# Gate products among the linear mixers, norms inside the output loop, and five smaller moves in a two-block decoder

## The reference

```python
h = rms_norm(x) * (1.0 + scale) + shift                 # modulation from c @ w_ada
(qa, ka, va, lra, ga, qb, fb, ib, gb, qc, kc, vc, gc) = split_columns(h @ w_in)
log_alpha = log_sigmoid(lra @ w_gla_gate2 + b_gla_gate) / 16
o_a = rms_norm(chunk_gated_linear_attn(qa, ka, va, log_alpha)) * gla_norm_w * silu(ga)   # "a", 512 wide
o_b = rms_norm(chunk_gated_linear_attn(silu(qb), k_b, ib, log_f)) * hgrn_norm_w * silu(gb)  # "b", 256 wide
o_c = stick_breaking_attn(qc, kc, vc) * silu(gc)                                          # "stick", 256 wide
x = x + gate * (concatenate([o_a, o_b, o_c]) @ w_out)
x = rms_norm(x) * final_norm_w
```

```python
x = x + memory_cross_attention(rms_norm_2(x, norm_cross), ...)
x = x + hierarchical_moe(rms_norm_2(x, norm_ffn), ...)   # router, then 32 experts of 512
return rms_norm_2(x, norm_final)
```

## Time and profile before

| | |
|---|---|
| median of 3 runs | 2309.74 (2307.14 to 2310.19) |
| the profiled execution, its own time | 2315.48 |
| its span, first to last instruction | 2313.6 |
| mean granted TensorE clock | 0.959 |
| PE, DVE, ACT, POOL busy | 93%, 37%, 24%, 11% of the span |
| last slices (experts): DMA | 408 to 414 GB/s |

### The profile page before, as it was taken

The page is one execution under the profiler, slowest core; times in us unless marked ns, Lnnn a source line. Parts: engine busy times, 40 slices in busy tenths (PEclk is TensorE's granted clock), DMA queues, the critical chain, the costliest instruction groups (busy, mean ns, idle before and its releaser), DMA issues.

```text
span 2313.6 us, 38071 instructions
## 1 busy us (share of the span) xinstructions
PE 2144.2 (93%) x15826; PEld 1198.3 (52%) x15826; DVE 863.6 (37%) x1488; ACT 552.5 (24%) x1002; POOL 249.7 (11%) x252
## 2 busy tenths in 40 slices
PE   6998899887998998999999899999899999999997
PEld 4445555555333443654445544466556666666553
DVE  2206630654555341185545563124421111111114
ACT  3013222323652210144112311023111111111112
POOL 0005410442330000000000000000010000000002
PEclk9998999987998999999999999999899999999999
DMA  8121121104010206102110302010389999999995
GB/s 296 61 94 53 37 64 37 46 14 141 1 71 20 64 35 209 37 1 73 37 37 1 137 0 73 0 49 37 137 296 409 412 408 414 410 411 411 409 368 225
DMA packets 100149, 348.98 MB, mean 151 GB/s; under 512 B 18632, under 2 KB 48992, under 8 KB 87264
## 3 DMA queue, kind: packets, MB, share of 16 engines
q1 hardware_dynamic: 56496, 267.64, 29.6%
q0 software_dynamic: 14688, 54.53, 6.3%
q10 hardware_dynamic: 28880, 25.66, 3.4%
HBM read 308.75 MB, written 39.06 MB: 150 GB/s over the span
## 4 chain that ended last, share of the span: by engine, by line
PE 38%; DMA 9%; DVE 4%; issue 1%; ACTq 0%; ACT 0%; POOL 0%; POOLq 0%; DVEq 0%; PEldq 0%
PE bank L590 17%; PE bank L1167 9%; DMA y_of_slot<-HT 9%; PE bank L1183 5%; PE bank L1001 2%; DVE work L1741 1%; PE bank L646 1%; PE bank L1173 1%; PE bank L1158 1%; PE bank L1253 1%; DVE HT L1776 1%; ACTq L1669 0%; PE bank L975 0%; ACT work L1277 0%; PE bank L1107 0%
## 5 line engine op out<-in xcount | busy, mean ns | idle before, releaser
L590 PE MATMUL bank<-slots,HT 128*128 128x512 f32 (+3 forms) x1216 | 427.2, 509 | 3.6 <-DVE HT L1776 1.9
L590 PE MATMUL bank<-HT,slots 128*128 128x512 f32 x736 | 320.8, 598 | 3.8 <-PEq L580 1.3
L590 PEld LDWEIGHTS bank<-slots,HT 128*128 128x128 f32 x1216 | 213.7, 195 | 196.6 <-issue 187.9
L1277 ACT ACTIVATE work<-bank 128x512 f32<-128x512 f32 (+5 forms) x215 | 114.4, 537 | 506.1 <-PE bank L590 352.5
L590 PEld LDWEIGHTS bank<-HT,slots 128*128 128x128 f32 x736 | 141.0, 192 | 181.3 <-issue 176.5
L1277 ACT ACTIVATE work<-work 128x1024 f32<-128x1024 f32 (+7 forms) x199 | 160.3, 817 | 246.7 <-DVEq L141 161.1
L1277 ACT ACTIVATE HT<-bank 64x256 f32<-64x256 f32 (+2 forms) x234 | 100.7, 435 | 462.5 <-PE bank L1167 221.6
L1167 PE MATMUL bank<-slots,HT 128*32 128x256 f32 x3264 | 179.5, 379 | 2.3 <-DVE HT L2366 1.2
L2446 POOL TENSOR_TENSOR work<-work 128x1024 f32<-128x1024 f32 (+4 forms) x84 | 137.0, 1630 | 379.6 <-DVEq L141 313.0
L1167 PE MATMUL bank<-work,HT 128*32 128x256 f32 x3072 | 168.9, 379 | 0.0
L1167 PEld LDWEIGHTS bank<-slots,HT 128*32 128x32 f32 x3264 | 107.6, 110 | 72.3 <-issue 6.1
(11 more groups left out here) (260 smaller groups left out, 2349.4 us busy)
## 6 DMA issues: line engine op xcount, KB each, us to landing
slots<-in_w_e_gate_dram SPq DMA_DIRECT2D x17, 2048.0 KB, 18.1
slots<-in_w_e_up_dram SPq DMA_DIRECT2D x17, 2048.0 KB, 22.7
slots<-in_w_e_down_dram SPq DMA_DIRECT2D x17, 2048.0 KB, 23.4
work<-in_w_e_gate_dram SPq DMA_DIRECT2D x16, 2048.0 KB, 18.0
work<-in_w_e_up_dram SPq DMA_DIRECT2D x16, 2048.0 KB, 22.7
work<-in_w_e_down_dram SPq DMA_DIRECT2D x16, 2048.0 KB, 23.5
slots<-in_w_in_dram SPq DMA_DIRECT2D x9, 2048.0 KB, 8.1
y_of_slot<-HT ACTq DMA_DIRECT2D x132, 96.0 KB, 23.4
```

The lines of the kernel that those rows point to most:

```text
L590: ins = pe.matmul(bank, lhsT, rhs, start=(n == 0), stop=(n == len(pairs) - 1))
L1277: return act.activation(o, i, f, bias=bias, scale=scale, **more)
```

## The change

1. *Gates of a made ahead.* `a_gate`'s products leave the output stage. Two tiles are made in `linear("a")`, six in `linear("b")`; each of the four pairs now has 56 products ahead (before 48, 48, 32, 32). All of them go to one HBM tensor, `products_ahead`.
2. *Where stick's inputs live.* Q and K come back through the weight slots as a chunk (`stick_qk`); the values go to `HT[:, 4:6]`, the gates of a to `HT[:, 0:4]`, of b to `HT[:, 6:8]`, all loaded by SP after the chunk `out1`, in pieces of 128 columns. The gates of stick follow when the linear stages are over, the chunk `att_q` when the stick stage is.
3. *Log-sigmoid under values.* The running sums' loop becomes a function, `running_sums(pair)`. `a_rank` comes before `a_v`; the bias products stand behind the first tile of values, seven tiles follow. Copies of values move behind the log-sigmoid on ACT and behind the running sums of the first pair on DVE, in a and b.
4. *Norms in the output loop.* Mean squares of tiles 0 and 1 are taken at the end of the stick stage and rooted with Ln and Exp; the other tiles' norm is `mix_normed(i + 2)` inside the loop over tiles. The gates of a and b lie in HT by tile columns (`gates[:, :, i * P:(i + 1) * P]`) and are multiplied as before; the norm weights `gla_w`, `hgrn_w` (now one column each) are applied in ACT's copy of the turned tile.
5. The router products of a step stand behind the turn of tile n-3; ACT squares a tile before it copies logits.
6. POOL waits for the first gathered block before it issues the second gather.
7. `BY_DVE = (2, 5, 7)`.

```diff
         add_chunk("a_qk_still")
+        add_chunk("a_rank", (w_in, 1024, 1040))
         add_chunk("a_v", (w_in, 512, 1024))
-        add_chunk("a_rank", (w_in, 1024, 1040))
         for n in range(4, 6):
             add_chunk(f"ada{n}", (w_ada, 512 * n, 512 * n + 512))
         add_chunk("c_qk", (w_in, 2576, 3088))
         add_chunk("c_gate", (w_in, 3344, 3600))
+        add_chunk("a_gate", (w_in, 1040, 1552))
         add_chunk("b_qf", (w_in, 1552, 2064))
         add_chunk("b_v", (w_in, 2064, 2320))
+        add_chunk("a_gate_still")
         add_chunk("cv_bgate", (w_in, 3088, 3344), (w_in, 2320, 2576))
-        add_chunk("a_gate", (w_in, 1040, 1552))
+        ahead_dram = scratch("products_ahead", [P, 28 * HALF])
+        add_chunk("stick_qk", (cut(ahead_dram[:, 0:4 * T], NK), 0, HALF))
...
-                 "b": [("cv_bgate", i, None) for i in range(NT)]}
-        AHEAD_CALLS = {"a": (8, 4, 4, 4, 4, 4, 4, 4, 3, 2, 7), "b": (6, 3, 3, 3, 3, 3, 3, 3, 2, 1, 2)}
+                 + [("c_gate", m, half) for m in range(2) for half in range(2)]
+                 + [("a_gate", i, None) for i in range(2)],
+                 "b": [("cv_bgate", i, None) for i in range(NT)] + [("a_gate", i, None) for i in range(2, NT)]}
+        EVEN = (6, 5, 5, 5, 5, 5, 5, 5, 4, 4, 7)
+        AHEAD_CALLS = {"a": (EVEN, (12, 8, 4, 4, 4, 4, 4, 4, 3, 3, 6)), "b": (EVEN, (11, 8, 4, 4, 4, 4, 4, 4, 4, 3, 6))}
         AHEAD_FIRST = {"a": 0, "b": len(AHEAD["a"])}
         ahead_over = {"a": [], "b": []}
-        AHEAD_GATES = 4 * T
-        AHEAD_ROWS = AHEAD_GATES + 4 * HALF
-        ahead_dram = scratch("stick_inputs", [P, AHEAD_ROWS + NT * HALF])
+        GATES_AHEAD = cut(ahead_dram[:, 4 * T:4 * T + 4 * HALF], 4)
+        A_AHEAD = [(0, 2, cut(ahead_dram[:, 12 * HALF:14 * HALF], 2)), (2, NT, cut(ahead_dram[:, 22 * HALF:28 * HALF], 6))]
+        B_AHEAD = cut(ahead_dram[:, 14 * HALF:22 * HALF], NT)
...
+        A_GATES, B_GATES = HT[:, 0:4, :], HT[:, 6:8, :]
...
+            ranked = ringA.filled
+            product_tm("a_v", 512, tm_fills()[0:1])
+            pe.wait_ge(ringA.free, ranked)
             Q, K, G, V, E, Qe, Ke, S = lin_area()
             for m in range(2):
                 for half in range(2):
                     ringV.close(pe.matmul(ringV.open(pe), Ke[0][0:RANK, m * P:(m + 1) * P],
                                           Ke[1][0:RANK, half * HALF:(half + 1) * HALF], start=True, stop=True))
+            product_tm("a_v", 512, tm_fills()[1:])
...
+            stick_over.append(4 * phases[0])
+            idle_products(banks[7], 5)
+            hear("dve")
+            turn_tile(0, O[:, 0, :], ringA, SB0 // P)
+            turned = [ringA.filled]
             for i in range(NT + 1):
+                if i + 1 < NT:
+                    hear("dve")
+                    turn_tile(i + 1, O[:, i + 1, :], ringA, SB0 // P)
+                    turned.append(ringA.filled)
                 if i < NT:
-                    product_tm("a_gate", 512, [(i, ringA)])
+                    pe.wait_ge(ringA.free, turned[i])
+                    for name in ("out0", "out1"):
+                        w = weights(name)
+                        ringV.close(chain(ringV.open(pe), [(mixed(k, i), w[:, k, :]) for k in range(NK)]))
+                        used(name)
                 if i:
                     hear("dve")
-                    turn_tile(i - 1, O[:, i - 1, :], ringA, SB0 // P)
-            emptied()
-            projected(("out0", "out1"), NORMED, 1, mixed)
+                    turn_tile(i - 1, NORMED[(i - 1) % 2], ringV)
...
-                for i in ROUTED_AT.get(n, ()):
-                    pe.wait_ge(ringV.free, turned_banks[i])
-                    router_product(i, ringA)
                 if n >= 3:
                     normed_ready.hear(pe)
                     turn_tile(n - 3, NORMED3[n % 3], ringV)
                     turned_banks.append(ringV.filled)
+                for i in ROUTED_AT.get(n, ()):
+                    pe.wait_ge(ringV.free, turned_banks[i])
+                    router_product(i, ringA)
...
+            do(rstd[:, 0:16], rstd[:, 0:16], ACT.Ln)
+            do(rstd[:, 0:16], rstd[:, 0:16], ACT.Exp, scale=-0.5)
             tell("dve")
-            hear("dve")
-            do(rstd[:, :], rstd[:, :], ACT.Sqrt)
+            def silu_gates(i0, i1):
+                do(A_GATES[:, :, i0 * P:i1 * P], A_GATES[:, :, i0 * P:i1 * P], ACT.Silu)
+                do(B_GATES[:, :, i0 * P:i1 * P], B_GATES[:, :, i0 * P:i1 * P], ACT.Silu)
+            def turned_mix(i):
+                for k0, k1, w in ((0, 4, gla_w), (4, SB0 // P, hgrn_w)):
+                    empty(lambda b: func(HT[:, k0:k1, i * P:(i + 1) * P], cut(b, 4)[:, 0:k1 - k0, :], ACT.Identity, scale=w))
+            act.wait_ge(a_gates_in, 16 * 8)
+            act.wait_ge(b_gates_in, 32)
+            silu_gates(0, 2)
             tell("dve")
-            for i in range(NT + 1):
-                if i < NT:
-                    if i >= len(A_GATES):
-                        hear("dve")
-                    empty(lambda b: func(A_GATES[i % len(A_GATES)], b, ACT.Silu))
+            act.wait_ge(stick_gates_in, 16)
+            do(STICK_GATES[:, 0:4:2, :], STICK_GATES[:, 0:4:2, :], ACT.Silu)
+            tell("dve")
+            turned_mix(0)
+            silu_gates(2, NT)
+            do(STICK_GATES[:, 1:4:2, :], STICK_GATES[:, 1:4:2, :], ACT.Silu)
+            tell("dve")
+            for i in range(NT):
+                if i + 2 < NT:
+                    hear("dve")
+                    r = rstd[:, 8 * i + 16:8 * i + 24]
+                    do(r, r, ACT.Sqrt)
                     tell("dve")
-                if i:
-                    turned_tile(i - 1, SB0 // P)
-            for i in range(NT):
+                if i + 1 < NT:
+                    turned_mix(i + 1)
...
+            def mean_squares(i):
                 o = O[:, i, 0:SB0]
                 tt(sq, o, o, ALU.mult)
                 line(dve.tensor_reduce(ssh[:, i, 0:4], cut(sq[:, 0:NG], 4), AX_X, ALU.add))
                 line(dve.tensor_reduce(ssh[:, i, 4:8], cut(sq[:, NG:SB0], 4), AX_X, ALU.add))
-            ts(rh[:, :, 0:4], ssh[:, :, 0:4], 1.0 / GLA_DV, EPS, ALU.mult, ALU.add)
-            ts(rh[:, :, 4:8], ssh[:, :, 4:8], 1.0 / HGRN_DV, EPS, ALU.mult, ALU.add)
-            line(dve.reciprocal(rstd[:, :], rstd[:, :]))
+                ts(rh[:, i, 0:4], ssh[:, i, 0:4], 1.0 / GLA_DV, EPS, ALU.mult, ALU.add)
+                ts(rh[:, i, 4:8], ssh[:, i, 4:8], 1.0 / HGRN_DV, EPS, ALU.mult, ALU.add)
+            for i in range(2):
+                mean_squares(i)
...
+            def stick_gated(c):
+                for pair in range(2):
                     o = stick_output(pair, c)
                     tt(o, o, cut(STICK_GATES[:, 2 * pair + c, :], 4), ALU.mult)
-            hear("act")
-            for i in range(NT):
-                for at, n, dv, w in ((0, 0, GLA_DV, gla_w), (NG, 4, HGRN_DV, hgrn_w)):
+            def mix_normed(i):
+                if i == 2:
+                    hear("act")
+                if i >= 2:
+                    mean_squares(i)
+                    line(dve.reciprocal(rh[:, i, :], rh[:, i, :]))
+                    tell("act")
+                    hear("act")
+                for at, n, dv, gates in ((0, 0, GLA_DV, A_GATES), (NG, 4, HGRN_DV, B_GATES)):
                     o = cut(O[:, i, at:at + 4 * dv], 4)
                     tt(o, o, bcast(rh[:, i, n:n + 4].unsqueeze(2), [P, 4, dv]), ALU.mult)
-                    tt(o, o, bcast(w.unsqueeze(1), [P, 4, dv]), ALU.mult)
-                hear("act")
-                tt(O[:, i, 0:NG], O[:, i, 0:NG], A_GATES[i % len(A_GATES)], ALU.mult)
-                tt(O[:, i, NG:SB0], O[:, i, NG:SB0], B_GATES[:, i, :], ALU.mult)
+                if i == 0:
+                    hear("act")
+                for at, n, gates in ((0, 4, A_GATES), (NG, 2, B_GATES)):
+                    o = cut(O[:, i, at:at + n * P], n)
+                    tt(o, o, gates[:, :, i * P:(i + 1) * P], ALU.mult)
+                if i == 4:
+                    stick_gated(1)
                 tell("pe")
-                if i + len(A_GATES) < NT:
-                    tell("act")
+            hear("act")
+            mix_normed(0)
+            hear("act")
+            stick_gated(0)
+            mix_normed(1)
             dve.wait_ge(row_in, 32)
             dve.wait_ge(gate_in, 16)
             tt(gate_row, gate_row, BIAS_ROW, ALU.add)
             for i in range(NT + 1):
+                if i + 2 < NT:
+                    mix_normed(i + 2)
...
                 gather_block(x, XG[x], rows_gathered[x])
+                if x == 0:
+                    pool.wait_ge(rows_gathered[0], 16)
...
+                if n == chunk_of["stick_qk"]:
+                    for x in range(2):
+                        sp.wait_ge(stage_stored[x], 16 * 4)
+                if n == chunk_of["stick_qk"] + 3:
+                    sp.wait_ge(phase, stick_over[0])
```

(39 more changed lines are left out.)

83 lines of the change are left out of this document (30 added, 53 removed).

## The result

The changed kernel takes 2257.28 us (median of 4 runs, 2254.06 to 2263.28) beside 2309.97 for the kernel before (4 runs, 2307.14 to 2314.70): a ratio of 0.9768, 95% interval 0.9744 to 0.9791. I had said 2250 (2236 to 2272), faster with 0.96. The profiled execution took 2257.62, 1.5 above the 2256.1 at which the sum ended on that scale.

A forecast was written before the change was run, and what follows sets the result against it. PE, busy 93% of the span, was taken as the bound, so moved products gain only by filling its idle or low-clock time. Terms summed to -59.4: 2256.1 on the profiled execution, 2250 from the median 2309.74, range 2236 to 2272.

The forecast's parts named there:

- Values' stage: Stage before the first mixer: both waits and their low clock go, c_qk's load ends it; 78.6 to 70.3, -8.3.
- First mixer +5.5: First linear mixer: 16 products more (+13.8), partly filling waits and low clock; 154.13 to 159.6.
- second +8.6: Second linear mixer: 48 products more (+41.3), mostly filling waits and low clock; 144.95 to 153.5.
- Rival 3: Mixers: waits stay and the added products come on top (+55.1); whole 2291, chance 0.07.
- Start of the stick mixer -2.4: Stick mixer's start: wait for Q and K shrinks (-4.9), a new wait for the values comes (+2.5).
- time to need 13.9, time to landing 16.2: Stick mixer's values: PE needs them after 13.9, loads land after 16.2; wait 2.3, taken as 2.5.
- Output stage -57.4: Output stage: gate products and norm wait leave, DVE sets the pace at 16.0 a tile; 204.2 to 146.8.
- Rival 1: Output loop stays on PE's pace, 15.3 a tile; stage 141 (-5.8), whole 2242 with values in time; chance 0.15.
- rival 4: Output loop runs in series, 29.4 a tile; stage 248 (+44), whole 2352; the slower case, chance 0.03.
- Rival 2: Transfers collide at phase ends: bias row up to 9.6 later (+8), values' wait +3; whole 2261, chance 0.20.
- Cross loop -6: Cross loop: turn ahead of the router product removes or shrinks waits and low clock; -6, ends -2 and -8.
- Tile 7, +0.6: Tail: adding tile 7 on DVE puts 2.61 on an engine with some 2 idle; +0.6, ends -1 and +2.

The follow-up runs named there:

- e3: Changed kernel with the row product of ada4 (chunk and product) put between the rank product and the values; ratio 0.976 to the kernel before.
- e13: Changed kernel with the stick mixer's values moved in pieces of 1024 bytes instead of 512; one run, 2253.72 us.
- e1: Changed kernel with the stick mixer's values issued ahead of out0 and out1 in SP's queue instead of behind them; 2249.65 us, ratio 0.9729 to the kernel before.
- e2: Changed kernel with POOL issuing the bias row and norm row ahead of the loads of x at the output stage's start; ratio 0.9786 to the kernel before.
- e10: e2 with squares and means of tile i + 3 put in VectorE's two waits for ACT's root of tile i; 2252.81 us, ratio 0.9763 to the kernel before.
- e6: Kernel before with only the cross loop's reordering (router products behind the turn, ACT's squares ahead of its logits copy); 2308.04 us, ratio 0.9987.
- e14: Changed kernel with the second gather issued at once behind the first, not after its landing; one run, 2260.29 us.
- e4: Changed kernel with the same 112 and 112 products ahead dealt out otherwise over the mixers' places; 2244.49 us, ratio 0.9712 to the kernel before.
- e5: Changed kernel with 42 of a_gate's 48 products left out of the second linear mixer (output not the reference's); one run, 2244.24 us.
- e11: Kernel with all edits: changed kernel plus those of e1, e3, e4, e10, and stick_gated(1) moved to tile 2; 2227.14 us, ratio 0.9636 to the kernel before.
- e12: As e11, with PE adding tile 7 instead of VectorE; 2222.69 us, ratio 0.9617 to the kernel before.

## Why the prediction was right, and where it was not

By step, as the prediction put them:

- **Values' stage: right in kind, 1.6 short.** (The prediction's own terms, 62 and 8.1, add up to 70.1, not the 70.3 it used.) Both waits and their low clock went and `c_qk`'s load became the end (e3 takes it away). 71.87, not 70.3: the load landed 9.35 after the last tile's product, not 8.1.
- **First mixer +5.5, second +8.6: the direction right, both too dear.** +2.9 and +4.0. The waits are the ones named, 2.72 and 0.16 (2.8 and 0.2), 2.08 (2.2), 2.94 (3.1). What failed is the low clock that I put behind each: the scores after the 2.72 run in 2.02, at full clock. Behind the 5.65 it is there (12 records in 8.28, else 5.39), and behind the wait ahead of the second pair's transposes (six records in 4.38 and 3.96, else 2.74). So the low clock was 4.7 and 1.8 where I had 7.7 and 6. Rival 3, 2291, falls with the 6.9 that the 55 of products cost.
- **Start of the stick mixer -2.4: the largest miss, measured +4.8 in that stage's length** (114.15 to 118.92), of which 5.5 of the old wait lies ahead of it (6.68 to 1.20); net -0.7. The wait is 6.70, above the 0 to 5 that I gave. Two parts of the term "time to need 13.9, time to landing 16.2" were off. Need was 5.0 + 1.2 + 5.5 = 11.7 (the first products now run at full clock: 0.93, not 1.65). Landing was 17.9 after the last product of HT; 512-byte pieces at 290 GB/s, not 391, make 0.9 of the 1.7 more. The rule of the Trainium skill (DMA: Bandwidth & Descriptors, Specifications), that 512 bytes is enough for line rate, does not hold here: 290 at 512, 350 at 1024 (e13), 390 to 412 for the weights' 2048. e1 shows that the order was the larger part.
- **Output stage -57.4: measured -56.4 (147.79 for 146.8).** Product 1 came at 26.0, as said; the tiles then took 15.3, 18.1, 16.3, 15.8, 16.2, 14.7 (said: 16.0, with one of 17.4). I gave the right pace with the wrong reason: "DVE sets the pace" says a full engine. The 10.5 that I called DVE's present work was a tile's time less one wait only; it still held DVE's waits for ACT's roots, which the kernel before has as well. Timeline of DVE of the kernel before, in one tile:

```profile
804.74 0.15 DVE L1744 TENSOR_SCALAR small<-small 128x1 f32<-128x1 f32 x1 [1.32 <-ACTq L141]
...
808.17 0.15 DVE L1744 TENSOR_SCALAR small<-small 128x1 f32<-128x1 f32 x1 [1.42 <-ACTq L141]
```

  It was the chain from product to epilogue to norm to turn, with 2.8 of idle in it (e2, e10). Two signs that I named failed with it: DVE was to have no idle (it is busy for 61%), and PE was to wait at each third turn (it waits at two turns of the loop, 2.00 and 0.48). Rival 1, the loop at PE's pace, came only with e10 (15.3 a tile), rival 4 not at all.
- **Rival 2, the collision: the bias row landed 14.8 after its issue, not 12.5.** So it came 2.3 later beside the small pieces of `att_q` (3.9 in e1), far from the 9.6 of even sharing and near the 1.5 for which the prediction shows no working. That speaks for the change between queues packet by packet that the Trainium skill (DMA: Bandwidth & Descriptors, Queues, rings and completion order) states; no run took `att_q` away. In the changed kernel product 0 still covered it, in e1 no longer.
- **Cross loop -6: measured -5.2 and, alone, -4.9 (e6).** In five later executions of the same code it took 152.2, which is -3.8. Tile 7, +0.6: between 1 and 3, not settled. Second gather 0: right (e14).
- **The scale.** The sum hit the profiled execution within 1.5, yet the median lies 7.0 above my figure, because I carried the 5.74 between the profile of before and its median over to the kernel after. e6 shows where such excess lay: in the start and the two mixers, the very stages that the change rebuilt. That an excess in a replaced stage doesn't survive is how I read this one pair of profiles.

Several errors cancelled, so the sum's 1.5 is luck in part: the mixers 7.2 better than said, against values' stage 1.6, stick mixer 1.7, output stage 1.0, cross loop 0.8 and some 4 in stages left alone and the tail. Of these 4 the expert stage's 1.4 is less than that stage varies by itself (last section). The second mixer, 148.93, also fell outside the 150 to 157 that I had named as a sign, on the cheap side.

## What to carry to other kernels

Work that is moved under waits costs only what the waits don't hold, so take the chain's pace from a place without waits and deal the moved pieces to the waiting places alone; dealing them out otherwise (e4) was worth 14.8 in the two mixers, more than any other edit here. Count also what the moved work holds up by the buffers it reads: here that delayed a load by as much (6.8) as the products cost in their own stage (6.1, e5). Before an engine is called the pace, add its idle inside the loop: where it waits for another engine's answer while it has work in hand for a later tile, that work goes into the wait (5 for two moved lines). And when a load is delayed by a freed buffer, give the first place in the queue to what is needed first: a megabyte behind four cost 6.3, the order alone.

## What the runs showed of the hardware

- The expert stage, the same code in all kernels, took 572.2 to 579.3 over 14 profiled executions, from the first expert product to the start of the last idle products, at 394 to 397 GB/s as a mean of the stage. In the changed kernel an expert takes 17.0 to 17.5 in the first two thirds, and five of the last ten take 17.9 to 19.1; what sets the long ones is not settled. This is the largest part of the scatter between profiles, and why stage lengths told apart what whole runs could not.
- The granted clock fell without an idle of PE inside the stretch. Window of the kernel with all edits, the first of the values' seven tiles:

```profile
117.68:130.00 12.32, 12.32 (x24) 5.42 (x24) 2.84 (x4) 9.50 (x9) 0.00 (x0) 0.79 0.00 0
130.00:140.00 10.00, 10.00 (x24) 4.37 (x23) 5.83 (x11) 0.60 (x1) 4.23 (x2) 1.00 0.00 0
```

PE is busy 12.32 of 12.32 at a mean of 0.79, a mix of its levels of 1.2 and 2.4 GHz, and at 1.00 in the same stretch of the kernel without tile 7 on VectorE; the wait ahead, 2.49 and 2.46, was the same. The seven tiles took 48.3 in eight of the twelve kernels with the change and 50.0 to 50.9 in the other four.
- Behind the same wait the clock was low in some executions and not in others. Timeline of PE in the cross loop, the changed kernel, then e2, which has the same code there:

```profile
1565.07 1.09 PE L1113 MATMUL bank<-cst,work 128*128 128x128 f32 x8 [0.89 <-DVEq L143]
```

```profile
1564.04 1.97 PE L1113 MATMUL bank<-cst,work 128*128 128x128 f32 x8 [0.89 <-DVEq L143]
```

This is where the loop's 150.8 and 152.2 part. The same shows in the output stage (e11 and e12, 1.7) and at the end of the second mixer (e3, 1.7). A difference of 1.4 to 2.5 between two single profiles can be this alone.
